# Sparse layer: compressed heads projected once, compression in plain fp32 from the ring in 32-column strips

## The reference, cut to what matters

```python
p = hn @ o_w_in[i]
q, kc, vc, ks, vs, kw, vw, gl, bg, cg, hd = _split(p, ...)   # kc, vc: 2 heads x 64
idx = np.arange(n_cmp)[:, None] * CMP_STRIDE + np.arange(CMP_LEN)[None, :]   # 15 windows
def compress(z, pos, w1, w2):
    zb = z[:, idx] + pos[None, None, :, None, :]
    zb = zb.transpose(0, 3, 1, 2, 4).reshape(bsz, C_KV_HEADS, n_cmp, CMP_LEN * C_HEAD_DIM)
    return jax.nn.gelu(zb @ w1) @ w2
k_cmp = compress(kc, pos_k, ck1, ck2)
v_cmp = compress(vc, pos_v, cv1, cv2)
```

## Time and profile before

| | us |
|---|---|
| runs | 2033.47, 2031.47, 2030.33 (median 2031.47) |
| span of the profiled execution | 2030.1 |
| PE / PEld busy | 1980.9 (98%) / 1745.5 (86%) |
| DVE busy | 1551.0 (76%) |
| ACT busy | 1152.5 (57%) |
| POOL busy | 396.7 (20%) |
| DMA | 401.21 MB, mean 198 GB/s |

### The profile page before, as it was taken

One profiled execution on the slowest core, in us unless ns is written; L12 is line 12 of the kernel. 1 busy time (PEld: TensorE's weight loads), 2 busy tenths in 40 slices (PEclk: granted clock), 3 DMA queues, 4 the chain that ended last, 5 costly groups with the idle time before them and its releaser, 6 DMA issues.

```text
span 2030.1 us, 31723 instructions
## 1 busy us (share of the span) xinstructions
PE 1980.9 (98%) x11697; PEld 1745.5 (86%) x11697; DVE 1551.0 (76%) x2173; ACT 1152.5 (57%) x1707; POOL 396.7 (20%) x192
## 2 busy tenths in 40 slices
PE   8999998999999999999999999999999999999997
PEld 6888998988888889988889898888998788888885
DVE  6777886777777769677768767777787798888886
ACT  5445564544554464654456535544566777777775
POOL 2222032322222210222322341332002100000000
PEclk9999999999999999999999999999999999999998
DMA  9555431555555554355544004655553688888894
GB/s 353 188 188 193 162 121 63 180 194 189 183 186 189 193 178 156 134 190 194 187 148 166 20 1 154 209 186 186 189 201 131 240 316 318 333 320 328 326 333 182
DMA packets 73395, 401.21 MB, mean 198 GB/s; under 512 B 8256, under 2 KB 8384, under 8 KB 41152
## 3 DMA queue, kind: packets, MB, share of 16 engines
q1 hardware_dynamic: 72848, 398.07, 56.4%
q10 hardware_dynamic: 432, 1.57, 0.2%
HBM read 398.57 MB, written 1.05 MB: 197 GB/s over the span
## 4 chain that ended last, share of the span: by engine, by line
PE 84%; DVE 9%; PEld 3%; ACT 2%; issue 1%; DMA 0%; SPq 0%; ACTq 0%; DVEq 0%; PEldq 0%
PE psum L798 20%; PE psum L322 13%; PE psum L323 12%; PE psum L324 12%; PE psum L778 10%; DVE w_lo L290 2%; PE psum L1032 2%; PE psum L555 2%; PE psum L1020 2%; PE psum L567 2%; PE psum L3123 1%; PE psum L557 1%; DVE w_lo L296 1%; PE psum L2379 1%; PE psum L1011 1%
## 5 line engine op out<-in xcount | busy, mean ns | idle before, releaser
L290 DVE TENSOR_TENSOR w_lo<-ring,w_hi 128x1024 fp32r<-128x1024 f32 x498 | 739.1, 1514 | 174.9 <-ACT w_hi L283 173.6
L283 ACT ACTIVATE w_hi<-ring 128x1024 fp32r<-128x1024 f32 x744 | 739.9, 1051 | 207.8 <-PEq L516 107.8
L296 POOL TENSOR_TENSOR w_lo<-ring,w_hi 128x1024 fp32r<-128x1024 f32 x132 | 325.8, 2468 | 1100.2 <-ACT w_hi L283 1100.2
L798 PE MATMUL psum<-fT,w_hi 128*128 128x512 f32 x1760 | 422.6, 392 | 3.8 <-ACT w_hi L283 3.8
L798 PEld LDWEIGHTS psum<-fT,w_hi 128*128 128x128 f32 x1760 | 330.8, 189 | 72.2 <-ACT w_hi L283 4.2
L322 PE MATMUL psum<-w_hi,hT_hi 128*128 128x512 f32 (+3 forms) x656 | 241.7, 369 | 3.8 <-DVE hT_lo L1346 2.0
L322 PE MATMUL psum<-w_hi,act_hi 128*128 128x512 f32 x596 | 234.2, 393 | 0.8 <-DVE act_lo L3403 0.8
L778 PEld LDWEIGHTS psum<-fT,w_lo 128*128 128x128 f32 x1760 | 226.0, 191 | 8.9
L323 PE MATMUL psum<-w_lo,act_hi 128*128 128x512 f32 x596 | 233.4, 392 | 0.0
L324 PE MATMUL psum<-w_hi,hT_lo 128*128 128x512 f32 (+3 forms) x656 | 232.3, 354 | 0.0
L324 PE MATMUL psum<-w_hi,act_lo 128*128 128x512 f32 x596 | 232.1, 389 | 0.0
(11 more groups left out here) (519 smaller groups left out, 2671.5 us busy)
## 6 DMA issues: line engine op xcount, KB each, us to landing
ring<-in_stream SPq DMA_DIRECT2D x249, 1024.0 KB, 5.4
ring<-in_stream SPq DMA_DIRECT2D x248, 512.0 KB, 4.3
tables<-in_tables SPq DMA_DIRECT2D x1, 2261.0 KB, 20.1
gain_row<-in_gains ACTq DMA_DIRECT2D x3, 512.0 KB, 4.5
rows<-in_rows SPq DMA_DIRECT2D x1, 1288.0 KB, 22.6
X<-in_x SPq DMA_DIRECT2D x1, 1024.0 KB, 4.9
result<-X SPq DMA_DIRECT2D x2, 512.0 KB, 3.4
columns<-in_columns SPq DMA_DIRECT2D x1, 993.0 KB, 15.2
```

The costliest lines, as they stand in the source:

```text
L283: act.activation(part(w_hi, g, i), ring[:, k, i * PART:(i + 1) * PART], ACT.Copy) \
L290: dve.tensor_tensor(part(w_lo, g, i), ring[:, k, i * PART:(i + 1) * PART], part(w_hi, g, i).bitcast(F32), ALU.subtract) \
L296: pool.tensor_tensor(part(w_lo, g, 2), ring[:, k, 2 * PART:STEP], part(w_hi, g, 2).bitcast(F32), ALU.subtract) \
L798: pe.matmul(psum[:, 4 + 2 * (s % 2) + o, :], w[0][:, o, k, :], fT[:, k, :, :].rearrange("p a c -> p (a c)"), start=k == 0, stop=False, ski ...
```

## The change

1. **Projection.** kc and vc are projected once, as two tiles in place of four; DVE writes each head's two copies from the one tile (four copies of 64 partitions per tile). The transposed tiles go from 16 to 14, in five steps ("tttt" and one "v" of two tiles) in place of six. The stream is one step shorter.
2. **Windows.** `n_zb` stays in plain fp32; its split into hi and lo is gone, and `windows` waits for the first transposed step alone.
3. **Compression.** Each block is one plain fp32 matmul with a 32-column stationary operand, straight from `ring`. Block l of 16 goes to the 32 output partitions of strip l % 4, so four blocks in a row address four strips. Nothing of these three steps is split; ACT and DVE instead wait for PE's end of each step and raise the split counters, which SP's loads wait for.
4. **Fold.** ACT copies all 128 rows of the sums. A plain fp32 matmul with a 0/1 table `sum32` adds the four strips and turns them at once, and Gelu comes after that, on `n_hid`.
5. **Order.** The Gelu table is loaded before the compression, the Exp table after the folded Gelu, ahead of `exps(2)`. The split of the first output step moves from the end of the compression to behind `exps(2)` on ACT and behind `largest(1)` on DVE. `tap(1)` of the convolution moves ahead of `largest(2)`.

```diff
-SPARSE_K, SPARSE_T, SPARSE_C = 3, 6, 3
+SPARSE_K, SPARSE_T, SPARSE_C = 3, 5, 3
-            n_zb_hi, n_zb_lo = ([take(f"n_zb_{n}{i}", [P, 16 + 3, 2, CMP_PAD], F32R) for i in range(2)] for n in ("hi", "lo"))
+            n_zb = [take(f"n_zb{i}", [P, 16, 2, CMP_PAD]) for i in range(2)]
-        N_KINDS = "k" * SPARSE_K + "t" * (SPARSE_T - 1) + "u"
+        N_KINDS = "k" * SPARSE_K + "t" * (SPARSE_T - 1) + "v"
-            if c < 4:
-                z = n_z[c // 2]
-                return [(z[0:64, c % 2, :], b[0:64, 0:SEQ]), (z[64:P, c % 2, 0:SEQ - 1], b[64:P, 1:SEQ])]
+            if c < 2:
+                z, heads = n_z[c], [slice(64 * kv, 64 * kv + 64) for kv in range(2)]
+                return [place for kv in range(2) for place in ((z[0:64, kv, :], b[heads[kv], 0:SEQ]), (z[64:P, kv, 0:SEQ - 1], b[heads[kv], 1:SEQ]))]
...
+                k, n = in_ring(g, g)
+                raw = ring[:, k, :].rearrange("p (q c) -> p q c", q=12)
+                pe.wait_ge(early_loaded[k], 16 * n)
                 for block_ in range(12 * s, min(12 * s + 12, 32)):
                     which, l = divmod(block_, 16)
-                    if block_ % 4 == 0:
-                        wait_part(pe, g, block_ % 12 // 4)
+                    if block_ % 12 == 8:
+                        pe.wait_ge(late_loaded[k], 16 * n)
...
-                    ins = three_passes(pe, b[:, 0:2 * P], windows, [x[:, block_ % 12, :] for x in w], l == 0, l == 15)
+                    strip = slice(2 * CMP_PAD * (l % 4), 2 * CMP_PAD * (l % 4 + 1))
+                    ins = pe.matmul(b[strip, 0:2 * P], n_zb[which][:, l, :, :].rearrange("p h n -> p (h n)"), raw[:, block_ % 12, :],
+                                    start=l < 4, stop=l >= 12, skip_group_check=True)
...
-                    ins = pe.transpose(b[:, 2 * CMP_PAD * i:2 * CMP_PAD * (i + 1)], n_rows[:, which, i * P:(i + 1) * P], ident[0:2 * CMP_PAD, 0:2 * CMP_PAD])
+                    ins = pe.matmul(b[:, 2 * CMP_PAD * i:2 * CMP_PAD * (i + 1)], n_rows_[:, which, i * P:(i + 1) * P], table("sum32"), start=True, stop=True)
...
-                does(f"used sparse hid {which}", n_rows[:, which, :], bank(f"sparse hid {which}")[0:2 * CMP_PAD, 0:2 * P], ACT.Gelu_apprx_tanh)
+                does(f"used sparse hid {which}", n_rows_[:, which, :], bank(f"sparse hid {which}")[:, 0:2 * P], ACT.Copy)
...
-            split_hi(act, c0 + 1, c0 + 1)
+            act.activation(warm[:, :], eps, ACT.Gelu_apprx_tanh)
             turned_units(0)
-            split_hi(act, c0 + 2, c0 + 2)
-            hidden(0)
-            split_hi(act, c0 + SPARSE_C, c0 + SPARSE_C)
+            for s in range(SPARSE_C):
+                if s == SPARSE_C - 1:
+                    hidden(0)
+                act.wait_ge(*after(f"sparse c {s} last"))
+                act.nop().then_inc(hi_ready, 2)
+                act.nop().then_inc(hi_last_ready, 1)
             hidden(1)
-            act.activation(warm[:, :], eps, ACT.Exp)
             for which in range(2):
                 act.wait_ge(*after(f"sparse hid turned {which}"))
                 does(f"used sparse hid turned {which}", n_hid[which].rearrange("p i c -> p (i c)"),
-                     bank(f"sparse hid turned {which}")[:, 0:4 * CMP_PAD], ACT.Copy)
+                     bank(f"sparse hid turned {which}")[:, 0:4 * CMP_PAD], ACT.Gelu_apprx_tanh)
+            act.activation(warm[:, :], eps, ACT.Exp)
             exps(2)
+            split_hi(act, c0 + SPARSE_C, c0 + SPARSE_C)
             act.wait_ge(*after("sparse kcmp"))
```

More of the change, by code:

```diff
@@ L2149, in sparse_vector @@
             for which in range(2):
-                for x in (n_zb_hi, n_zb_lo):
-                    does(None, dve.memset, x[which][:, 16:, :, :].bitcast(F32), 0.0)
+                does(None, dve.memset, n_zb[which][:, :, :, CMP_N:], 0.0)
             does("sparse kcmp clear", dve.memset, n_kcmp[:, :, :], 0.0)
@@ L2162, in windows @@
             def windows():
-                wait_proj(dve, "sparse", N_KINDS, range(SPARSE_K, SPARSE_K + 2))
-                for which in range(2):
-                    does(None, dve.memset, n_zb[which][:, :, :, CMP_N:], 0.0)
+                wait_proj(dve, "sparse", N_KINDS, range(SPARSE_K, SPARSE_K + 1))
                 for which, pos in enumerate(("pos_k", "pos_v")):
@@ L2170, in windows @@
                         for a in range(2):
-                            does(None, dve.tensor_tensor, n_zb[which][:, 8 * a:8 * a + 8, kv, 0:CMP_N],
+                            does(f"sparse zb {which}", dve.tensor_tensor, n_zb[which][:, 8 * a:8 * a + 8, kv, 0:CMP_N],
                                  z[:, :, a:a + CMP_N, 0], wide(col(pos)[:, 8 * a:8 * a + 8], CMP_N), ALU.add)
-                settle()
-                for which in range(2):
-                    does(None, dve.tensor_copy, n_zb_hi[which][:, 0:16, :, :], n_zb[which][:, :, :, :])
-                settle()
-                for which in range(2):
-                    does(f"sparse zb {which}", dve.tensor_tensor, n_zb_lo[which][:, 0:16, :, :], n_zb[which][:, :, :, :],
-                         n_zb_hi[which][:, 0:16, :, :].bitcast(F32), ALU.subtract)
             def squared_row():
@@ L2204, in weights @@
                 does(f"sparse p {i}", dve.tensor_tensor, blocks(S), blocks(S), wide(r.rearrange("p u b -> p (u b)"), P), ALU.mult)
-            proj_copies_vector(dve, "sparse", at, N_KINDS, n_place, ahead=True, lasts=range(len(N_KINDS)), row_at=1, scale_of=n_scale,
+            proj_copies_vector(dve, "sparse", at, N_KINDS, n_place, lasts=range(len(N_KINDS)), row_at=1, scale_of=n_scale,
                                later={3: lambda: (squared_row(), rotate(0)), 4: lambda: rotate(1), 5: windows, 7: lambda: weights(0)},
@@ L2210, in sparse_vector @@
             c0 = first_step[at] + len(N_KINDS)
-            split_lo(dve, c0 + 1, c0 + 1)
-            split_lo_last(dve, c0 + 1, c0 + 1)
-            split_lo(dve, c0 + 2, c0 + 2)
-            split_lo_last(dve, c0 + 2, c0 + 2)
             tap(0)
             settle()
-            split_lo(dve, c0 + 3, c0 + 3)
-            split_lo_last(dve, c0 + 3, c0 + 3)
+            for s in range(SPARSE_C):
+                dve.wait_ge(*after(f"sparse c {s} last"))
+                k, n = in_ring(c0 + s, c0 + s)
+                dve.wait_ge(late_loaded[k], 16 * n)
+                dve.nop().then_inc(lo_ready, 2)
+                dve.nop().then_inc(lo_last_ready, 1)
+            tap(1)
             largest(2)
@@ L2222, in sparse_vector @@
                 does("sparse hv", dve.tensor_copy, n_hv[:, i, :, :], over(n_hid[1][:, i, :], 4))
-            tap(1)
             largest(1)
+            split_lo(dve, c0 + 3, c0 + 3)
+            split_lo_last(dve, c0 + 3, c0 + 3)
             dve.wait_ge(*after("sparse vcmp"))
@@ L3666, in stream_steps @@
             gl = w[:, 1280:1304].reshape(-1, 8, 3)[:, SLOT_HEADS].transpose(0, 2, 1).reshape(-1, 24)
[L3667 removed]
             yield from column_steps([q, w[:, 768:1280], gl], SPARSE_K)
[L3669 removed]
+            yield from column_steps([w[:, 512:768], w[:, 1816:], w[:, 1304:1816]], SPARSE_T)
             tiles = np.concatenate([by_row_tile(a["nsa_cmp_k_w1_2"][0]), by_row_tile(a["nsa_cmp_v_w1_2"][0])], axis=1)
```

27 lines of the change are left out of this document (10 added, 17 removed).

## The result

Slower, by a little: 2034.46 us median of 20 runs (2033.29 to 2039.26) against 2031.55 us of before (2029.89 to 2034.70), ratio 1.0018 with a 95% interval of 1.0012 to 1.0024. The forecast was 2024.4 us. The profiled run has a span of 2031.6 us, before 2030.1 us.

The account below looks back on a forecast made before the run. PE was taken to bound the projection and compression, and DVE's arrival at the vcmp product the tail. Gains of 4.1 and 8.1 less 5.1 us give 7.1, from 2031.5 to 2024.4 us; 8-in-10 range 2021.5 to 2028.2.

Parts of the forecast that it names:

- compression begins earlier: Projection: two tiles fewer on PE gain 5.44 us, DVE's extra copies return 1.3, so compression starts 4.1 us earlier.
- compression shorter: Compression: 32 plain fp32 blocks in four concurrent strips take 4.6 us in place of 12.7, gaining 8.1 us.
- end of blocks to n_rows longer: Tail: fold 0.6, Exp table load 1.4 and output-step split on DVE 3.1 give back 5.1 us.
- that product: The vcmp product on DVE in the sparse stage's tail, starting at n_rows; its shift was taken to move the end equally.
- if the mixture of experts changes its length: Later stage: one listed sign that the prediction is wrong, given without a size.
- four strips at once: Compression: four 32-column strips run concurrently at 0.22 us a pass, judged from a trace row with two strips; chance 0.60.
- The 1.3 us that the projection gives back: Projection: DVE makes nine copies where six stood, has no slack, so 1.3 us lands on PE.
- Rival 1: Compression: only two strips run at a time, blocks 6.9 us not 3.5, ending at 2027.8 us; chance 0.13.
- rival 2: Compression: strips run in series, 14.9 us against 12.7, ending slower at 2034.7 us; chance 0.05.
- give nothing of themselves: Projection: the four removed splits (3.42 us DVE, 2.96 ACT each) lie beside PE work not waiting for them, gaining nothing.
- Rival 3: Tail: PE idling brings a half-clock stretch, doubling the second half of scores(1), 1 to 2 us, 2025.4 to 2026.4; chance 0.12.
- Rival 4: Tail gives back less: DVE meets the split early or ACT's exponentials hide it, 2 to 3 us stay, 2021.9; chance 0.10.

Follow-up runs that it names:

- own_sum: The change, but DVE makes the 32-column table in a tile at the end of the sparse stage's tiles, nothing else shifted: 2024.93 us, ratio 0.9970 to the kernel before.
- layout: The kernel before plus the 32-column table loaded and read by nobody, shifting all tiles behind it by 128 bytes: 2041.98 us, ratio 1.0053.
- sbuf_only: The kernel before with an unused 32-column tile behind the tables in SBUF, loads and HBM arrays unchanged: 2041.37 us, ratio 1.0047.
- dram_only: The kernel before with 32 more table columns in HBM, not loaded, SBUF unchanged: 2030.53 us, ratio 0.9997.
- all_shift: The kernel before with the unused 32-column tile ahead of the ring, so all tiles move 128 bytes together: 2032.60 us, ratio 1.0001.
- ht_shift: The kernel before with the unused 32-column tile between X and hT_hi, so hT and all behind it move 128 bytes: 2032.16 us, ratio 1.0001.
- proj_alone: The kernel before with only the projection part of the change, compression in three passes, tables as before: 2031.52 us, ratio 1.0002.
- own_split: own_sum with the output step's split moved earlier, ACT's behind the second hidden bank's copy, DVE's ahead of largest(1): 2025.68 us, ratio 0.9971 to the kernel before.
- comp_alone: The change without its projection part (heads projected twice, SPARSE_T 6), tables still 32 columns wider: 2040.27 us, ratio 1.0043 to the kernel before.
- pad_step: The change plus one more step of zeros in the stream, so the mixture of experts begins at step 160: 2038.95 us, ratio 1.0038 to the kernel before.
- own_one_strip: own_sum with all 32 compression blocks in the first strip, one behind the other, and the fold over it alone: 2034.67 us, ratio 1.0020 to the kernel before.

## Why the prediction was wrong, step by step

The forecast's arithmetic was for the sparse stage, and with the tiles unshifted it holds (own_sum, start of stage 0.30 us earlier than before):

| step | forecast | own_sum |
|---|---|---|
| compression begins earlier | 4.1 | 1511.99 - 1507.50 - 0.30 = 4.2 |
| compression shorter | 8.1 | 12.49 - 4.70 = 7.8 |
| end of blocks to n_rows longer | 5.1 | 14.48 - 9.28 = 5.2 |
| n_rows to the last turns | 0 | 13.87 - 13.78 = 0.1 shorter |
| stage | 7.1 | 6.9 |
| median | 2024.4 us | 2024.93 us |

- **Failed:** "All stages behind it are unchanged and each waits for the one before, so a shift of that product is a shift of the end." Their instructions are unchanged, but not their addresses. The new table was priced at nothing, and it is a 10 us term by itself (layout, sbuf_only). The miss is 2034.46 - 2024.4 = 10.1 us, and 9.5 us of it lie between own_sum and the change, which differ in where that table lies and in who makes it. The prediction's last sentence named the sign, "if the mixture of experts changes its length", but gave it no mechanism and no chance.
- Stage lengths against before, us, from the starts of the same matmuls in the profiled runs, show where it goes. The stretches are in the time of before. Left out are the feed-forward stages, and 290 to 360, 1040 to 1064 us and the end, where before itself has half-clock stretches (at 350, 1046 and 2016 us) that not every run has:

| kernel | delta 200-290 | attention 745-845 | rwkv 1064-1240 | sparse 1429-1552 | router 1552-1600 | experts 1600-2010 |
|---|---|---|---|---|---|---|
| dram_only | 0.0 | 0.0 | 0.0 | 0.0 | 0.0 | 0.1 |
| all_shift | 0.0 | 0.0 | 1.8 | 0.0 | 3.2 | 0.0 |
| ht_shift | 0.0 | 0.0 | 1.6 | 0.2 | 0.0 | 0.0 |
| own_sum | -0.7 | 0.0 | 0.2 | -6.9 | 0.0 | 0.0 |
| layout | 0.5 | 0.6 | 3.6 | 1.6 | 1.3 | 2.7 |
| sbuf_only | 0.7 | 0.2 | 3.8 | 1.6 | 1.5 | 2.8 |
| after | 0.7 | 0.5 | 2.3 | -5.3 | 1.7 | 2.8 |

  The experts' 2.7 us of layout is pace, and so is the sparse stage's 1.6. Of rwkv's 3.6 us 0.9 is pace, and the rest and the router's 1.3 are half-clock stretches. The one in the router also came in executions with unshifted tiles (proj_alone, own_split, all_shift: 1.5 to 3.2 us), so it isn't the layout's alone; the one at 1108 us came in layout, sbuf_only, comp_alone, pad_step and after, but in all_shift and ht_shift too. What puts them there stays open, and so does which pair of tiles costs the 3 ns. The feed-forward stages, whose matmuls read fT and w from the same group, keep their pace in every kernel (226.7 ns between starts at 380 to 540 us).
- **Right:** four strips at once, by the nearest row's two (4.70 us; serial 14.87 in own_one_strip). The 1.3 us that the projection gives back to DVE's copies (own_sum loses 1.25 us against before between 1463 and 1500 us). Rival 1 and rival 2 are out as causes; rival 2 came near the result, 2034.7, for a wrong reason, and own_one_strip is that rival at 2034.67.
- **Right as a sum only:** 4.1 and "8.1 less 5.1" are not two terms that each stand alone. The forecast argued that the four splits that go "give nothing of themselves". They do: without that, PE waits 2.5 us for `weights(0)` (proj_alone).
- **Rival 3, the clock:** one stretch in the tail in after and in own_sum (from 1520.9 us); it doubled the second half of `scores(1)`, in own_sum L1592 x4 0.81 us for 0.43. It costs 0.4 us there, and 0.7 us in after.
- **Rival 4:** DVE did not meet the split early; the tail gave back 5.2.
- **The noise:** the prediction held that 0.2% can't be told from no change. With 11 to 20 runs the intervals are 0.06 to 0.1% to each side, so the 0.2% of the result, 1.0018 (1.0012 to 1.0024), can be told from no change.

A version that beats both kernels came out of it: own_sum, 6.8 us faster than before and 9.5 faster than the change.

## What to carry to other kernels

Whatever is allocated ahead of others is an edit of all of them: price it by an unused tile of the same width in the kernel before, which is a cheap run. A small constant belongs behind all tiles, or is made where it is used. When a part is moved earlier, list what the other engines still owe at that point, since two parts of a change can pay only together; and before handing work to an idle engine or an earlier hole, ask which port it shares and when its input lands.

## What the runs showed of the hardware

- A shift of 128 bytes between two groups of SBUF tiles changes the pace of matmuls, start to start: 1% longer for the 512 columns of the experts, 4% longer for the 256 columns of the sparse projection, and 2.5% shorter (118 to 115 ns) for the 256 columns of the experts. The same shift of all tiles does none of this. The Trainium skill ("SBUF — State Buffer", SBUF: two separate sides) has TensorE never waiting for anyone at its ports. These runs do not show that it waits, but its pace is not free of where the operands lie: 229.4 against 232.0 ns.
- Four strips of 32 output columns in plain fp32 with 256 moving columns: 24 records in 1.48 us against 5.31 us in one strip, 3.6 times.
- A GpSimd instruction of 2.36 us held a DVE instruction of 0.16 to 0.18 us until it was over, and that three times (2.34, 2.28 and 1.79 us in place of 0.18, 0.17 and 0.16).
- Single half-clock stretches of 3.4 us, 1.5 us each where PE is the bound, stand in one kernel's profiled run and not in another's at the same place (the router: in proj_alone, not in before). The three slowest of own_sum's 11 runs (2028.5 to 2029.8 us) have a granted clock of 0.990 to 0.992, the others (2022.8 to 2025.2 us) 0.994 to 0.996, so that scatter goes with the clock.
